# Modulation sums over partitions: the partial sums stream through a matrix of ones, and each partition's two are picked out with the identity

## What is computed

```python
cond = jax.nn.silu(c)
for l in range(DEPTH):
    mod = (cond @ w_ada[l] + b_ada[l]).astype(x.dtype)[:, None, :]      # 1024 -> 6 * 1024
    sh1, sc1, g1, sh2, sc2, g2 = jnp.split(mod, N_MOD, axis=-1)
    h = _rmsnorm(x, norm1_w[l]) * (1.0 + sc1) + sh1
    x = x + g1 * _token_mixers(h, ...)
    h = _rmsnorm(x, norm2_w[l]) * (1.0 + sc2) + sh2
    x = x + g2 * _conv_ffn(h, ...)
# second network: c_silu = silu(c_2)
mod = c_silu @ w_ada + b_ada                                            # 1024 -> 3 * 1024
shift, scale, gate = jnp.split(mod, 3, axis=-1)
u = rms_norm(x, norm_g) * (1 + scale[:, None]) + shift[:, None]
```

## Time and profile before

| | |
|---|---|
| Time, median of 3 runs | 2828.22 us (2824.87 to 2830.96) |
| The profiled execution, its time | 2836.11 us |
| its span, first to last instruction | 2834.3 us |
| TensorE busy | 2709.0 us (96%), weight loads 2177.6 us |
| VectorE busy | 1814.7 us (64%) |
| ScalarE busy | 1153.0 us (41%) |
| GpSimd busy | 689.8 us (24%) |
| Mean granted TensorE clock | 0.972 of full speed |
| DMA | 302.6 MB, mean 107 GB/s |

### The profile page before, as it was taken

The page is one execution under the profiler, slowest core; times in us unless marked ns, Lnnn a source line. Parts: engine busy times, 40 slices in busy tenths (PEclk is TensorE's granted clock), DMA queues, the critical chain, the costliest instruction groups (busy, mean ns, idle before and its releaser), DMA issues.

```text
span 2834.3 us, 37110 instructions
## 1 busy us (share of the span) xinstructions
PE 2709.0 (96%) x14950; PEld 2177.6 (77%) x14950; DVE 1814.7 (64%) x2960; ACT 1153.0 (41%) x1900; POOL 689.8 (24%) x514
## 2 busy tenths in 40 slices
PE   7999899999999998999999999989999999999997
PEld 6877678888878676888886878767687788777686
DVE  6779759776577676876558768644436558545434
ACT  3133544333242454533324463344424464444422
POOL 0000046988700004356540032000110122000110
PEclk9899999999999998999999999999899999999899
DMA  8353034454432112344433435221222323221221
GB/s 255 104 168 106 29 104 141 163 177 157 149 110 68 58 59 82 126 136 155 141 119 103 151 110 157 75 64 53 75 95 81 91 68 93 80 86 53 75 91 65
DMA packets 281115, 302.60 MB, mean 107 GB/s; under 512 B 9968, under 2 KB 263024, under 8 KB 280944
## 3 DMA queue, kind: packets, MB, share of 16 engines
q1 hardware_dynamic: 267568, 250.21, 28.2%
q0 software_dynamic: 13088, 49.55, 5.3%
q10 hardware_dynamic: 288, 0.47, 0.1%
HBM read 289.97 MB, written 2.10 MB: 103 GB/s over the span
## 4 chain that ended last, share of the span: by engine, by line
PE 86%; DVE 7%; ACT 4%; issue 1%; DMA 1%; SPq 1%; DVEq 0%; ACTq 0%
PE ps L560 85%; PE ps L769 2%; DVE wl L1398 1%; DVE hl L1404 1%; DMA raw<-in_w_in 1%; DVE adaacc L1404 0%; DVE rawt L1404 0%; ACT recat L927 0%; SPq L1997 0%; ACT att_p L927 0%; DVE xT L1404 0%; DVE recat L1685 0%; ACT att_s L927 0%; ACT hh L927 0%; DMA t1s<-rawt 0%
## 5 line engine op out<-in xcount | busy, mean ns | idle before, releaser
L560 PE MATMUL ps<-hh,wh 128*128 128x512 f32 x2208 | 894.6, 405 | 25.1 <-DVE wl L1398 10.5
L560 PE MATMUL ps<-hh,wl 128*128 128x512 f32 x2208 | 870.8, 394 | 0.0
L560 PE MATMUL ps<-hl,wh 128*128 128x512 f32 x2208 | 870.4, 394 | 0.0
L1398 DVE TENSOR_TENSOR wl<-raw,wh 128x2048 fp32r<-128x2048 f32 (+3 forms) x234 | 495.1, 2124 | 214.3 <-ACT wh L927 214.1
L560 PEld LDWEIGHTS ps<-hh,wh 128*128 128x128 f32 x2208 | 419.7, 190 | 139.2 <-issue 39.6
L560 PEld LDWEIGHTS ps<-hh,wl 128*128 128x128 f32 x2208 | 419.7, 190 | 93.3
L560 PEld LDWEIGHTS ps<-hl,wh 128*128 128x128 f32 x2208 | 420.4, 190 | 81.7
L927 ACT ACTIVATE wh<-raw 128x2048 fp32r<-128x2048 f32 (+3 forms) x234 | 369.9, 1591 | 189.2 <-PE ps L560 172.1
L560 PE MATMUL ps<-fh,wh 128*128 128x512 f32 x432 | 171.6, 397 | 0.0
L1940 POOL TENSOR_TENSOR strewn<-strewn,cond 128x1024 f32<-128x1024 f32 x80 | 167.5, 2094 | 7.5 <-DMA strewn<-in_w_ada 5.8
L560 PE MATMUL ps<-fh,wl 128*128 128x512 f32 x432 | 168.3, 390 | 0.0
(11 more groups left out here) (288 smaller groups left out, 4171.3 us busy)
## 6 DMA issues: line engine op xcount, KB each, us to landing
raw<-in_w_in SPq DMA_DIRECT2D x75, 1024.0 KB, 5.3
raw<-in_w_up SPq DMA_DIRECT2D x46, 1024.0 KB, 5.2
strewn<-in_w_ada POOLq DMA_DIRECT2D x80, 512.0 KB, 4.2
raw<-in_w_ada SPq DMA_DIRECT2D x24, 1024.0 KB, 5.3
raw<-in_w_in SPq DMA_DIRECT2D x44, 512.0 KB, 5.3
raw<-in_w_out SPq DMA_DIRECT2D x16, 1024.0 KB, 5.0
raw<-in_w_down SPq DMA_DIRECT2D x16, 1024.0 KB, 4.9
stage<-in_w_ada SPq DMA_DIRECT2D x8, 1024.0 KB, 11.5
```

Source lines behind the costliest of these rows:

```text
L560: return e.matmul(o, a, b, start=start, stop=stop, skip_group_check=True)
L1398: return e.tensor_tensor(o, a, b, op)
```

## The change

TensorE's sum becomes one matmul with the matrix of ones (128x128) as weights and all 256 columns of `adaacc` as the moving operand, in fp32. Every partition of the bank then holds all 256 sums. VectorE multiplies columns 0 to 255, seen as two groups of 128, with the identity, broadcast over the two groups, into columns 256 to 511 of the same bank, and reduces each group with an add, which leaves partition p its two sums. For the 68 chunks that have a bias the add follows in place as a third instruction. Each waits for the one before it. The four chunks of the start take the identity as loaded, and ScalarE's rounding of it waits for the last of them; all later ones take the rounded copy. The quick chunks keep their form in a function of their own. The planner's costs stay, and so does the order.

```diff
+    def diagonals(self, b, eye):
+        sums, own = (b[:, c:c + 256].rearrange("p (x t) -> p x t", x=2) for c in (0, 256))
+        return sums, own, eye.rearrange("p (x t) -> p x t", x=1).broadcast_to([128, 2, 128])
@@ tensor_program, adasum
-        mm(b[:, 0:1], acc[:, 0:128], M.ones[:, 0:1], True, True)
-        mm(b[:, 1:2], acc[:, 128:256], M.ones[:, 0:1], True, True).then_inc(*up("pe_ada", ("sums", chunk_)))
+        mm(b[:, 0:256], M.ones, acc[:, :], True, True).then_inc(*up("pe_ada", ("sums", chunk_)))
@@ scalar_program, loaded
         go.wait_ge(*at("loaded", "c1"))
+        go.wait_ge(*at("mods", (1, 0, 3)))
@@ vector_program
+    def own_sums(chunk_, dst, eye):
+        sums, own, mask = M.diagonals(bank("ada", chunk_), eye)
+        go.wait_ge(*at("sums", chunk_))
+        tt(own, sums, mask, ALU.mult).then_inc(*up("dve_mod"))
+        go.wait_ge(*last("dve_mod"))
+        e.tensor_reduce(dst, own, mybir.AxisListType.X, ALU.add).then_inc(
+            *up("dve_mod", ("out", ("ada", chunk_)), ("mods", chunk_)))
+
     def adasum(chunk_):
         which, l, j = chunk_
+        eye = M.cst[:, C_ID:C_ID + 128]
+        if chunk_ not in [p["chunk"] for p in X.first]:
+            go.wait_ge(*at("rounded"))
+            eye = M.ident
         if which == "shift":
-            go.wait_ge(*at("sums", chunk_))
-            e.tensor_copy(M.shifted(chunk_[1:]), bank("ada", chunk_)[:, 0:2]).then_inc(
-                *up("dve_mod", ("out", ("ada", chunk_)), ("mods", chunk_)))
+            own_sums(chunk_, M.shifted((l, j)), eye)
             return
         dst, bias, per = (M.mod1, "bada", 48) if which == 1 else (M.mod2, "bada2", 24)
         col = l * per + 2 * j
-        go.wait_ge(*at("sums", chunk_))
-        tt(dst[:, col:col + 2], bank("ada", chunk_)[:, 0:2], M.vec(bias, col, 2), ALU.add).then_inc(
-            *up("dve_mod", ("out", ("ada", chunk_)), ("mods", chunk_)))
+        own_sums(chunk_, dst[:, col:col + 2], eye)
+        go.wait_ge(*last("dve_mod"))
+        tt(dst[:, col:col + 2], dst[:, col:col + 2], M.vec(bias, col, 2), ALU.add).then_inc(*up("dve_mod", ("mods", chunk_)))
```

## The result

The changed kernel takes 2845.62 us (median of four runs, 2843.27 to 2848.90) beside 2829.52 of the kernel before: a ratio of 1.0051, 95% interval 1.0034 to 1.0069. A second set of eight runs, on another occasion, gave 1.0030 (1.0019 to 1.0041). The forecast was 2841.6 us, +13.4; measured are +16.1 and +8.5 (0.0030 x 2829.85). So the time and the sign came out as forecast. The terms of the sum did not, as the experiments show: the TensorE part of the change, forecast at +5.5 us, gives back about 11, and VectorE's part, forecast at +7.9, costs about 20.

What follows compares the result with a forecast made beforehand. The prediction took TensorE, busy 96% of the span, to bound the kernel. TensorE's 5.5 us plus 7.9 us of waits for VectorE made 13.4 us on 2828.2, so 2841.6 us, range 2831 to 2856.

Steps and rivals of the forecast that it cites:

- the pair under 0.46 us: Sign of being wrong: the new sum's two fp32 instructions on TensorE cost under 0.46 us, where 0.54 was forecast.
- the clock moved by over 0.003: Sign of being wrong: the granted clock of the execution moves by over 0.003.
- TensorE's sum: TensorE's stream: a new sum takes 0.54 us, 0.08 more than the old; 5.5 us for 69 sums, between -1 and +19.
- the addition of 0.1 us for the way back to ordinary weights: Step in TensorE's price: about 0.1 us for returning to ordinary weights, on top of 0.44 us for two 256-column instructions.
- a rival with 0.04: TensorE's clock: longer sum streams keep it at its upper level; 2820 us if nearly all comes back; chance 0.04.
- The opposite rival: First block: longer TensorE waits bring another low-clock stretch; one of 10 us costs 5, giving 2847 us; chance 0.12.
- VectorE's instructions: After each sum: multiply 0.418, reduce 0.424, then the add, instead of one 0.151 us add; some 65 us more VectorE.
- Waits, in all: TensorE's added waits for VectorE: start 2.0, first block 2.65, two sums in one place 3.2; together 7.9 us.
- Start: First four shift chunks: TensorE waits longer for h in rounds two to four (0.35, 0.3, 1.35), first hidden; 2.0 us.
- First block: Adds at 190.43 and 219.29 and the wl at 271.34 delay TensorE by 0.9, 1.05 and 0.7; 2.65 us.
- Two sums in one place: Two adds ahead of one wl: 1.8 us at 456.60, 0.7 near 614, 0.7 in the second feed-forward stretch; 3.2 us.
- All other sums 0 now: Other feed-forward sums cost TensorE nothing, slack to the chunk's use being over 1 us; thirteen in the last blocks also 0.

Runs made afterwards that it cites:

- e2: Kernel before with only the new 256-column matmul; VectorE adds the bias to the first two columns, pick left out, so values are wrong; ratio 0.9961.
- e5: Kernel before with one extra new-form 128x256 matmul ahead of each chunk's two old ones, its result not read; ratio 1.0081.
- e6: Kernel before with each chunk's two one-column matmuls done twice, the first time into unused columns of the bank; ratio 1.0129.
- e10: Kernel before with 128 columns of ones instead of one streamed through each accumulator as weights, same result, no pick; 2820.3 us, ratio 0.9965.
- e12: Kernel before with 128 columns of ones in only the first seven sums of TensorE, one column in the other 66; ratio 0.9982.
- e3: Changed kernel with the old one-column matmuls put back, VectorE's three instructions kept in full size on their two columns; ratio 1.0074.
- e4: Kernel before with VectorE's one add of a sum cut into a copy from the bank to SBUF and a bias add in SBUF; ratio 1.0008.
- e7: The changed kernel itself, timed and profiled again in a second set of eight runs; ratio 1.0030.

## Why the prediction came out right, and where it did not

- **Total and sign**: 13.4 us forecast, 16.1 and 8.5 measured, both inside 2831 to 2856. Right, but by errors that cancel, so by luck as far as the mechanism goes. One of the prediction's own signs of being wrong came in full (the pair under 0.46 us), and one in the first set of runs only (the clock moved by over 0.003: 0.9692, against 0.9734 to 0.9739 of the kernel before; 0.9734 in the second set).
- **TensorE's sum**, forecast 0.54 us and +5.5: 0.44 us, nothing in its own length. The failed step is the addition of 0.1 us for the way back to ordinary weights; the two passes cost 0.44 with it. The prediction's estimate of 0.44 from the Trainium skill ("TensorE: Matmul & The Clock Gate", section "Back-to-back issue gap", with "FP8 and Floating Point Precision") agrees with the trace.
- **The clock**: the failed step of the whole. It was a rival with 0.04 (longer streams keep the clock up, worth up to 22 us), set aside because few sums lie near the slow stretches. e2, e5 with e6, and e10 are 10 to 12 us apart from the old form in time, and 7, 16 and 10 in the table's last column; e12 shows that seven sums are enough for a good part of it. The opposite rival, longer waits that bring more low clock, had 0.12 and one stretch of 5 us; e3 puts it at 12 us with the old matmuls, and the changed kernel less e2 at 7 us (75.5 - 68.6) or 19 us (87.5 - 68.6) with the new ones, by the set; single stretches of 1.7 us stand behind the longer waits near 457 and 1340. So the size of this term is known only roughly. A hint was in the kernel before: the matmuls drop to 0.63 us right behind the one-column sum of 91.40 and its wait.
- **VectorE's instructions**: multiply 0.423, reduce 0.424 as taken from the 0.418 and 0.424 of the earlier trace rows. The add was assumed to stay at 0.15; it was read from PSUM there, and is 0.53 out of SBUF. +69.6 us of VectorE where 65 were forecast; in e4 the wl behind the slow adds are shorter by nearly as much.
- **Waits, in all** 7.9 forecast, 8.7, 8.3 and 8.1 measured as TensorE's idle time (changed, e7, e3). The size was right, the places only in part. Start: 2.0 forecast, 3.0 measured as the sum of waits up to 100 us (27.1 against 24.1). There a wait of 1.56 us for h at 32.16 had been called hidden; the one at 59.79 grew by 0.9 us, not 1.35; a third, for recq, grew from 1.29 to 1.77. First block: 2.65 forecast, nothing measured (waits from 100 to 400 us: 21.9 and 22.0 in the two profiles, 21.9 before). Some waits grew there, such as those for stt from 2.7 to 4.4 us, and others shrank, such as those for reck from 3.1 to 1.7. Two sums in one place: 1.8 forecast near 457, 1.56 measured; 0.7 near 614, and no wait there.
- **"All other sums 0 now"**: fell at one of them (2.84 us at 1182.63), and the second feed-forward's double sum cost 1.95 where 0.7 was forecast. Both are the race: the slack was measured in time to the chunk's use, as if VectorE's instructions behind the sum kept their lengths. With 0.95 us more in front of it, the add or the wl meets a GpSimd instruction that it had beaten before. At the second place the second add starts at 1336.67, 0.13 us behind GpSimd's multiply; in the kernel before, the wl itself started 1.65 us ahead of it (1330.92 and 1332.57).
- **Waits and queues on ScalarE, POOL, DMA**: forecast at nothing; ScalarE 1153.6 against 1153.0 us busy, POOL 687.5 against 689.8, and nothing in the traces speaks against it.

Open: whether sums after the first seven bring part of e10's gain, and which; how a one-column matmul comes to cost clock; and why the changed kernel's clock was 0.969 in one set and 0.973 in the other. Nothing here varied these.

## What to carry to other kernels

Slack on an engine is only slack while the order with its rival for SBUF stays: before putting a microsecond in front of a long instruction with two SBUF inputs, look at what GpSimd starts in that microsecond. A short matmul in front of a wait is not free because it is short: where the granted clock falls behind it, try more columns through the same weights. Up to 128 took no time here, and the kernel gained 0.35%. And price an edit by its halves: two terms of 11 and 20 us can sum to what a wrong working says.

## What the runs showed of the hardware that was not expected

- An fp32 matmul pair with 1, 64 or 128 columns (four records, each with a weight load) takes 0.46, 0.45 and 0.44 us in the stream; one of 256 columns (two records) takes 0.44.
- Of the same length, one-column sums go with more time at TensorE's lower clock level: 74.7 us lost to it in the kernel before, 67.8 with 64 columns, 65.1 with 128 (one group of runs), and 82.3 with the one-column sums doubled (73.7 in its own group). The Trainium skill, "TensorE: Matmul & The Clock Gate", Part 1, says the default is throttled and activity releases it; e10 against the kernel before, sums equal in length and granted clock different (0.9769 and 0.9736), is in line with that.
- Waits of 1.8 to 3.0 us at two places were followed by a stretch at the lower clock level in every profile that had them, eight in all, 1.7 us lost each; waits of 0.9 to 1.6 us near 457 were not, in ten; a third wait of 2.7 to 2.8 us was in one profile of four.
- A VectorE add of 128x2 with both operands in SBUF takes 0.16 us, or up to 2.42 us until the GpSimd instruction under way, or starting within 0.5 us, has ended; out of PSUM it is 0.14 to 0.16 us. Multiply and reduce out of PSUM stay within 0.42 to 0.43.
- A multiply that also sums 128x128 is 0.35 us by its record, and two of them with their accumulator reads take 0.55 us of VectorE, against 0.92 for multiply and reduce of 128x256 and 0.15 for the add.
